# A two-layer diffusion block: the modulation product and the weight loads moved inside a one-core kernel

## What is computed

```python
sc, scc = silu(c), silu(c_ctx)
for l in range(DEPTH):                                   # DEPTH = 2
    mx = split(sc  @ w_mod[l] + b_mod[l], 6)             # w_mod: (2, 1024, 6144), 50.3 MB in all
    mc = split(scc @ w_mod[l] + b_mod[l], 6)
    px = project(modulate(rms_norm(x,  g_pre_mix[l]), mx[0], mx[1]), w_in[l], ...)
    pc = project(modulate(rms_norm(xc, g_pre_mix[l]), mc[0], mc[1]), w_in[l], ...)
    x  = x  + mx[2] * rms_norm(token_mix(px, keys of context and latents), g_post_mix[l])
    xc = xc + mc[2] * rms_norm(token_mix(pc, keys of context), g_post_mix[l])   # not in the last layer
    x  = x  + mx[5] * rms_norm(conv_ffn(modulate(rms_norm(x, g_pre_ffn[l]), mx[3], mx[4])), g_post_ffn[l])
    xc = xc + mc[5] * rms_norm(conv_ffn(...), g_post_ffn[l])                    # not in the last layer
```

## Time and profile before

| | us |
|---|---|
| median of three runs | 4011.78 |
| the profiled execution | 4007.81 |
| its span, first to last instruction | 4006.0 |
| TensorE busy in it | 3350.1 |
| VectorE busy | 2018.1 |
| ScalarE busy | 1232.3 |
| GpSimd busy | 716.9 |

### The profile page before, as it was taken

The page is one execution under the profiler, slowest core; times in us unless marked ns, Lnnn a source line. Parts: engine busy times, 40 slices in busy tenths (PEclk is TensorE's granted clock), DMA queues, the critical chain, the costliest instruction groups (busy, mean ns, idle before and its releaser), DMA issues. The chain is left out here.

```text
span 4006.0 us, 46136 instructions
## 1 busy us (share of the span) xinstructions
PE 3350.1 (84%) x16882; PEld 2586.9 (65%) x16882; DVE 2018.1 (50%) x2714; ACT 1232.3 (31%) x1830; POOL 716.9 (18%) x884
## 2 busy tenths in 40 slices
PE   5398968778684999999998498787876679999997
PEld 0187845555473888888886386655555567777775
DVE  1266546666342444544445465656663434444445
ACT  0143245555231221111212242455552221212121
POOL 0033434444101000000001132444441100000001
PEclk7598979999897999999999698999998889999999
DMA  9544210000346111111112444100003441111112
GB/s 382 201 165 165 86 51 28 27 29 7 115 156 191 42 39 45 37 31 37 37 42 80 163 169 152 64 18 29 26 7 115 174 130 42 52 42 52 42 47 105
DMA packets 200655, 342.64 MB, mean 86 GB/s; under 512 B 23864, under 2 KB 145920, under 8 KB 184672
## 3 DMA queue, kind: packets, MB, share of 16 engines
q1 hardware_dynamic: 200544, 341.20, 24.6%
HBM read 254.03 MB, written 87.13 MB: 85 GB/s over the span
## 5 line engine op out<-in xcount | busy, mean ns | idle before, releaser
L1911 DVE TENSOR_TENSOR ff_acc<-ff_dn,ff_acc 128x512 f32<-128x512 f32 x396 | 271.9, 690 | 328.1 <-PE ff_dn L123 327.8
L121 PE MATMUL ff_z_gate<-ff_hT,ff_u_hi 128*128 128x512 f32 (+1 forms) x880 | 331.6, 377 | 76.2 <-DMA ff_hT<-hT_d 76.2
L121 PE MATMUL ff_dn<-ff_d_lo,ff_a_hi 128*128 128x512 f32 x792 | 320.1, 404 | 32.7 <-issue 17.0
L123 PE MATMUL ff_z_gate<-ff_hT,ff_u_hi 128*128 128x512 f32 (+1 forms) x880 | 329.7, 375 | 0.0
L1796 POOL TENSOR_TENSOR ff_ms<-ff_ss,c_eps 128x1 f32<-128x1 f32 x18 | 19.8, 1101 | 1730.2 <-ACT ff_t_gate L1874 1730.2
L122 PE MATMUL ff_z_gate<-ff_hT,ff_u_lo 128*128 128x512 f32 (+1 forms) x880 | 328.8, 374 | 0.0
L121 PE MATMUL ff_z_value<-ff_hT,ff_u_hi 128*128 128x512 f32 (+1 forms) x880 | 327.1, 372 | 0.0
L123 PE MATMUL ff_z_value<-ff_hT,ff_u_hi 128*128 128x512 f32 (+1 forms) x880 | 326.6, 371 | 0.0
L122 PE MATMUL ff_z_value<-ff_hT,ff_u_lo 128*128 128x512 f32 (+1 forms) x880 | 325.7, 370 | 0.0
L1897 DVE SCALAR_TENSOR_TENSOR ff_t_gate<-ff_z_gate,c_vec,ff_t_gate 128x1023 f32<-128x1023 f32 (+1 forms) x132 | 132.1, 1015 | 362.9 <-ACT ff_t_gate L1849 356.1
L122 PE MATMUL ff_dn<-ff_d_hi,ff_a_lo 128*128 128x512 f32 x792 | 310.5, 392 | 0.0
(11 more groups left out here) (256 smaller groups left out, 7320.3 us busy)
## 6 DMA issues: line engine op xcount, KB each, us to landing
mod_wm<-in_w_mod_dram SPq DMA_DIRECT2D x48, 1024.0 KB, 7.9
ff_u_raw<-in_w_up_dram SPq DMA_DIRECT2D x88, 512.0 KB, 3.8
ff_d_raw<-in_w_down_dram SPq DMA_DIRECT2D x44, 512.0 KB, 4.4
hT_d<-fr_hs SPq DMA_DIRECT2D x20, 1024.0 KB, 5.0
kv_hs<-hT_d SPq DMA_DIRECT2D x20, 1024.0 KB, 4.8
hT_d<-mo_hs SPq DMA_DIRECT2D x18, 1024.0 KB, 6.0
ff_hT<-hT_d SPq DMA_DIRECT2D x18, 1024.0 KB, 10.9
st_stage<-in_w_in_dram SPq DMA_DIRECT2D x48, 256.0 KB, 3.7
```

Source lines behind the costliest of these rows:

```text
L121: e.matmul(out, w[0], x[1], start=start, stop=False)
L123: return e.matmul(out, w[0], x[0], start=False, stop=stop)
L1911: e.tensor_tensor(out, dn[:, half, :], out, ALU.add).then_inc(acc_done, 1)
```

## The change

The modulation product is split. `w_mod` of a layer has three groups of 2048 columns: group 0 holds shift 0 and scale 1, group 1 gate 2 and shift 3, group 2 scale 4 and gate 5. Group 0 of layer 0 is computed in a new phase `pre`, together with layer 0's constants. The other five groups (40 pieces of 1 MB) and layer 1's constants are computed inside layer 0's context attention `ac` by a helper `Late`, whose instructions stand between the attention's steps on each engine. Both `setup_phase` calls and `modulation_phase` are gone. The factors `c_ab`, the gain and lambda exist once per layer now, and only the gates are stored to DRAM. The bias enters through a small matmul with a selecting matrix, and the two vectors are padded to 32 columns.

The front's weight is loaded whole, in four pairs of row blocks, into the place where its `w_lo` will stand (`pair`), so no load waits for `w_lo`. In layer 0 these loads are issued by SP at the end of `pre`'s program, ahead of the barrier; in layer 1 at the start of the front. The key weight is loaded whole by two transfers in the middle of the front. The attention's small tiles move into the arena that the key weight used. In `ac` the score tiles shrink to 512 columns, which frees PSUM for the modulation.

```diff
-def modulation_phase(nc, c_in, c_ctx, w_mod, b_mod, mod_d):
...
-def setup_phase(nc, l, c, inp, mod_d, ident_in):
...
+class Modulation:
...
+    def load(self, e, n):
+        l, g = self.groups[n // KD]
+        if n >= self.ring:
+            e.wait_ge(self.w_used, n - self.ring + 1)
+        e.dma_start(self.wm[:, n % self.ring], self.w_v[l, g, n % KD]).then_inc(self.w_in[n % self.ring], 16)
+
+    def chunk(self, e, n):
...
+            for j in range(self.GRP):
+                r = (l * self.NG + g) * self.GRP + j
+                e.matmul(acc[32 * j:32 * j + 32, :], self.sel[0:24, r, :], self.bias[0:24, :], start=True, stop=False)
+        e.wait_ge(self.w_in[n % self.ring], 16 * (n // self.ring + 1))
+        for j in range(self.GRP):
+            ins = e.matmul(acc[32 * j:32 * j + 32, :], self.cs[0].act[:, k, :], self.wm[:, n % self.ring, j, :],
+                           start=False, stop=(k == KD - 1))
+        ins.then_inc(self.w_used, 1)
...
+class Late:
+
+
+    CALLS = 24
+
+    def __init__(self, ph, cs, inp, mod_d):
+        self.m = Modulation(ph, cs, inp, mod_d, [(0, 1), (0, 2), (1, 0), (1, 1), (1, 2)], 4, 2)
+        self.s = Setup(ph, 1, cs[1], inp)
+        self.chunks = [range(self.m.chunks * i // self.CALLS, self.m.chunks * (i + 1) // self.CALLS) for i in range(self.CALLS)]
+
+    def sync(self, e):
+        m = self.m
+        m.load_bias(e)
+        for n in range(m.chunks):
+            m.load(e, n)
+            if n == 4:
+                self.s.load(e)
+            if n % KD == 6 and n > KD:
+                m.store(e, n // KD - 1)
+        m.store(e, len(m.groups) - 1)
+        m.end(e)
...
+    def tensor(self, e, i):
+        if i == 3:
+            self.s.turn_rows(e)
+        if i == 5:
+            self.s.turn_ws(e)
+        for n in self.chunks[i]:
+            self.m.chunk(e, n)
+            if n % KD == 3 and n > KD:
+                self.m.turn_group(e, n // KD - 1)
...
+def pre_phase(nc, cs, inp, mod_d, first_loads):
...
+        @block.sync
+        def _(e):
+            for v, src in ((LATV, inp["c"].rearrange("b d -> (b d)")), (CTXV, inp["c_ctx"])):
+                e.dma_start(cond[:, :, v], src.rearrange("(k p) -> p k", p=P), allow_slow_non_contiguous=True).then_inc(cond_in, 16)
+            for n in range(KD):
+                m.load(e, n)
+            first_loads(e)
...
+        @block.tensor
+        def _(e):
+            e.wait_ge(act_done, 1)
+            for n in range(3):
+                m.chunk(e, n)
+            s.turn_rows(e)
+            m.chunk(e, 3)
+            s.turn_ws(e)
+            for n in range(4, KD):
+                m.chunk(e, n)
+            m.turn_group(e, 0)
...
+class QueryLoads:
...
+    def first(self, e):
+        for i in range(KD // 2):
+            if i < 2:
+                self.load_x(e, i)
+            for a, b, at in Q_COLS:
+                e.dma_start(self.w_raw[:, 2 * i:2 * i + 2, at:at + b - a], self.w_v[:, 2 * i:2 * i + 2, a:b]).then_inc(self.w_loaded[i], 16)
...
+class KeyLoads:
...
+    def first(self, e):
         for a, b, at in KV_COLS:
+            e.dma_start(self.w_raw[:, :, at:at + b - a], self.w_v[:, :, a:b]).then_inc(self.loaded, 16)
...
             for u in range(2):
                 load(0, u)
+            if late:
+                late.sync(e)
```

More of the change, by code:

```diff
@@ L143, in sb, with next_place, pair, within @@
         return self.ctx.enter_context(self.nc.sbuf_tensor(f"{self.name}_{name}", shape, dt))
+    def next_place(self):
+        return -(-self.nc.sbuf_base // 32) * 32
+    def pair(self, raw, rounded, shape):
+        base = self.next_place()
+        tile = self.sb(rounded, shape, F32R)
+        return self.nc.alloc_sbuf_tensor_at(f"{self.name}_{raw}", shape, F32, offset=base), tile
+    def within(self, arena):
+        at, end = arena[0], arena[0] + arena[1]
+        def place(name, shape, dt=F32):
+            nonlocal at
+            tile = self.nc.alloc_sbuf_tensor_at(f"{self.name}_{name}", shape, dt, offset=at)
+            at += 4 * int(np.prod(shape[1:]))
+            assert at <= end
+            return tile
+        return place
     def ps(self, name, shape, dt=F32):
@@ L397, in _ @@
         def _(e):
-            e.wait_ge(loaded, 16 * n_loads)
-            for i in range(3):
-                e.transpose(turn[:, i, :], rows[:, i, :], c.ident[:, :])
-            for g in range(BG):
-                ins = e.transpose(turn[:, 4 + g, :], ws[:, g, :], c.ident[:, :])
-            ins.then_inc(turned, 1)
+            e.wait_ge(act_done, 1)
[4 more added lines that the diff above has]
+            s.turn_ws(e)
@@ L431, in _ @@
-        @block.scalar
-        def _(e):
-            e.wait_ge(lam_done, 3)
-            e.activation(lam_exp[:, :], lam_sum[:, :], ACT.Exp).then_inc(exp_done, 1)
+            e.wait_ge(ident_in, 16)
+            m.select(e)
+            s.vector_rows(e)
+            s.vector_ws(e)
+            m.rows_out(e, 0)
+            m.to_ab(e, 0)
 def rope_steps(e, done, at, x, out, a, b, cs, sn, heads, width):
@@ L527, in store_ob @@
                 e.dma_start(y_d[tiles[i], :, AH * HD:AH * HD + BW], ob[:, i % 2, :]).then_inc(ob_stored[i % 2], 16)
-            load_x(0)
-            load_w(0)
-            load_w(1)
-            load_x(1)
-            for k in range(2, KD):
-                load_w(k)
+            if not loaded:
+                ql.first(e)
             e.dma_start(rope[:, :, :, :], rope_in.rearrange("t p a w -> p t a w")).then_inc(rope_in_s, 16)
@@ L931, in _ @@
             load(0)
-            for k in range(wr.RING, KD):
-                e.wait_ge(w_lo_done, k - wr.RING + 1)
-                wr.load(e, k)
             load(1)
@@ L1071, in _, with attention_phase @@
                 post_k(r)
[L1074 removed]
+def attention_phase(nc, l, c, name, b0, blocks, n_keys, q_d, y_d, stage, late_of=None):
     NK = n_keys * P
@@ L1184, in over_blocks @@
                 step(n, items(0, True, False))
+                if late and more:
+                    more(e, n)
             if blocks > 1:
@@ L1190, in over_blocks @@
                 step(n, items(blocks, False, True))
+                if late and more:
+                    more(e, STEPS + n)
         def map_of(n):
@@ L1329, in step @@
                     out_c(*item(unit, UNITS))
-            over_blocks(e, step)
+            over_blocks(e, step, late and late.tensor)
         @block.vector
@@ L1416, in step @@
                     pc_out(*item(n // 2 - 2, COMBS))
-            over_blocks(e, step)
+            over_blocks(e, step, late and late.vector)
         @block.gpsimd
@@ L1421, in _ @@
             PC = 4
+            if late:
+                late.gpsimd(e)
             def combine(i, k):
@@ L1522, in step @@
                     exp_c(*item(n, STEPS))
-            over_blocks(e, step)
+            over_blocks(e, step, late and late.scalar)
 def gates(ph, inp, mod_d, l, which_gate, g_name, G, g):
```

405 lines of the change are left out of this document (232 added, 173 removed).

## The result

After the change the median is 3894.61 us (four runs, 3891.73 to 3897.41) against 4012.27 (four runs, 4011.36 to 4014.14) of the kernel before on the same chip: a ratio of 0.9706, 95% interval 0.9689 to 0.9723, or 118 us less. The prediction said 3898 as the median. The profiled execution took 3891.73 us, its span is 3889.9, so 116.1 less than the 4006.0 of before.

The account below looks back on a forecast made before the run. It took the start to be bound by loads, with phases a serial chain and transfers pacing the modulation. Its terms summed to -113.5 us: median 4011.8 to 3898, forecast 3885 to 3904 (0.50), range 3872 to 3936.

Parts of the forecast that it names:

- Part 1: Start until the front's first load: at 42 us instead of 162.15, constants landing at 28; -120 us (-130 to -107).
- Rival A: At the start, constants land late (32 to 41 us) and hold back pieces; time 3902 to 3911, chance 0.27.
- Part 2: Front of layer 0: tokens and weights already there, last `w_lo` 20.4 us in, rope table issued first; -20 us.
- Part 5: Front of layer 1: weights loaded in one run without the ring, seven splits to 25.5 us; -15 us.
- Parts 3 and 4: Key weights of both layers are split earlier, -7 us; the setup of layer 1 goes, -16.5 us.
- Part 6: Context attention of layer 0: 40 pieces at transfer pace, 122 us instead of 56.6; +65 us.
- Rival B: TensorE, at 1.9 us per piece, sets the context attention's pace: 143 us or +86, time 3919; chance 0.15.
- Case C: In the context attention the ring runs dry each step, pieces load one by one: +281, time 4114; chance 0.03.
- Case D: Late phases shift through other places of tiles on chip, a few us; chance 0.05 with the rest, either direction.

## Why the prediction was right

The time came out right, and so did the wait behind each large term. The size of the first term is in part luck: two errors, of 7 and of 4 us, went against each other.

**Part 1, the start** (-120 predicted, -117.0 measured). The constants landed at 35.05, not at the 28 taken as the middle: +7. What follows them took 10.1 us and not 14: pieces 4 to 7 ran in 3.9 us and not 6.2, as they lay ready and the granted clock was high (0.95 us each, not 1.55), and from the end of the copy to the front's first load it took 2.0 and not 3.6. That is -3.9. Rival A was thus true as a mechanism (32 to 41 for the constants), though we had given it a chance of 0.27, and its time, front at 46 to 55, was missed by 1 us. The run with the constants first shows that they can be there at 14.1, the one without the front's loads that SP's later bytes hold them back by 4 us (31.1). "ACT's activation is out by about 11 us" was wrong: 19.5, since ACT's issues took 17.4 us and not 7.3. It cost nothing, as pieces 0 to 2 were done 9 us ahead of the constants. The rule that the prediction cited with rival A from the Trainium skill (DMA: Bandwidth & Descriptors, Queues, rings and completion order) speaks of engines that go round robin between queues. These runs agree with it, though none sets it against another way of sharing. Rival A's estimate of 32 was nearer to 35 than our 28.

**Part 2, the first front** (-20, -22.4). The last `w_lo` ends 19.8 us into the phase; we had 20.4. Part 5, layer 1's (-15, -15.2): 26.8 against 25.5. Both terms are of loads that wait for nothing. Putting the wait back in layer 1 cost 14.3 us there; layer 0 was not tested.

**Parts 3 and 4.** The key sides were to give -7 together and gave -3.7 and -6.3. Layer 1's setup was to give -16.5 and gave -16.3.

**Part 6, the context attention** (+65, +68.2). First piece at 10.4 (10.6 predicted), last at 113.8 (110), then 11.1 us of tail (12). From the first piece to the last it is 103.4 us. Of these the last 30 pieces, behind the gap, came 2.51 us apart, where we had 2.45 to 2.49; at 2.51 for all 39, 5.3 us are left for the gap and the constants, where we had 4.8. The prediction's own terms give 111 to 112.5 for the last piece and not 110, so part of the 3 us is a slip of its addition. Half the columns changed nothing, half the bytes took 20.8 us off. Rival B's 1.9 us per piece was seen at the start and the end of the phase; from 395 to 455 the clock was full (1.00) and a piece cost 0.95 to 1.06. What B would have cost is seen in the run with 64 rows. The Trainium skill gives 358 GB/s for HBM (DMA: Bandwidth & Descriptors, Specifications); by that figure the term would have been +84, an estimate. The 420 GB/s from 395 to 455 decide against it. That the same estimate had part 1 at -117 is chance: the pieces were not what set it. The Trainium skill also gives 435 as the width of the ports (DMA: Bandwidth & Descriptors, Where 436 GB/s comes from), and the rows approach that.

**The range.** Its ends, -131 and -76, do not both follow from its parts: the ends of parts 1 and 6 with the other terms give -130.5 and -79.5. The time lay inside either.

**Case C** did not come: the ring ran dry once, for the constants. A ring of two gave +34 over the change, or a context attention 102 us longer than before the change, where case C had +281.

**Case D, the late phases.** Instruction lists of `al`, `mo` and `ff` are the same, yet mixed output and latent attention together took 2.8 us more in layer 0, and 2 us less in layer 1, and the last phase 3.2 less. All are inside the range. Not all of it is spread: layer 0's mixed output took 192.2 us before and 195.2 to 196.5 in all thirteen traces since. Layer 1's took 160.4 before and 160.2 after. The cause is open.

## What to carry to other kernels

A bulk load that feeds little arithmetic belongs beside a phase that computes, and its price there goes by what that phase has to spare: a piece cost its transfer, 2.15 to 2.5 us, in a phase that waited for the DMA engines, and about its matmuls, 1.15, in one that TensorE filled and in which transfers had room. Ask where the DMA share is low and TensorE is busy, before filling the phase that merely looks idle. Small loads that gate work land late behind large ones. Sending them first brought them in 21 us earlier here and still gained nothing, because the large ones then came late; moving the work that needs them to the end of TensorE's order gained 6.6 us. And an engine that issues loads for the next phase holds the barrier until it has issued them.

## What the runs showed that we had not expected

- Issuing is not a constant 0.43 us. Once the large transfers are queued, SP's issues of the front's weights take 17.2 us for nine and ACT's last four 2.4 to 3.2 us each, from about 7 us on in both queues; with the constants first, ACT issued nine in 4.7 us. In that run SP's issue, and no engine's work, ended the phase.
- A load into 64 partitions moved 210 GB/s, the same bytes as half rows into 128 partitions up to 417.
- The granted clock was lower with smaller matmuls: in the context attention 0.83 after the change, 0.68 with 256 columns, 0.53 with 64 rows. So the pieces' matmuls fell only from 49.2 to 35.0 us with half the columns, and with 64 rows they rose to 72.0. Why the clock was lower was not tested.
